# A hybrid decoder block on one core: the residual taken from its normed form, and scatter and weight transposes moved between the gate and the up product

## What is computed

```
def reference(x, ...):
    h = rms_norm(x, g_mix); z = h @ w_in + b_in          # 1024 -> glu a, b | q | k | v | two gates
    y_conv = conformer_conv(glu_a, glu_b, ...)           # 31 causal taps per channel, layer norm, silu, @ w_conv_out
    y_attn = sliding_window_attention(q, k, v, sinks) @ w_attn_out + b_attn_out
    x = x + (gate_conv * y_conv + gate_attn * y_attn) @ w_out
    x = x + moe_ffn(rms_norm(x, g_ffn), ...)
    return rms_norm(x, g_final)

def moe_ffn(h, ...):                                     # 256 tokens, 32 experts, top 4
    logits = hf @ w_router + b_router
    top_v, top_e = lax.top_k(logits, TOP_K); top_w = softmax(top_v)
    ... # tokens sorted by expert; for the rows xblk of expert e:
        g = jnp.minimum(xblk @ w_gate[e] + b_gate[e], 7.0)
        u = jnp.clip(xblk @ w_up[e] + b_up[e], -7.0, 7.0)
        a = (u + 1.0) * (g * jax.nn.sigmoid(1.702 * g))
        yb = a @ w_down[e] + b_down[e]
    y = zeros.at[row_tok].add(yb * row_w)                # scatter, weighted

```

## Time and profile before

| | us |
|---|---|
| median of three runs | 1177.32 |
| the profiled execution, its own time | 1175.85 |
| its span (first to last instruction) | 1174.1 |
| PE busy | 1120.3 (95%) |
| PE weight loads busy | 530.4 (45%) |
| DVE busy | 325.5 (28%) |
| ACT busy | 179.7 (15%) |
| DMA, mean over the span | 376 GB/s, 441.69 MB |

### The profile page before, as it was taken

One profiled execution on the slowest core, in us unless ns is written; L12 is line 12 of the kernel. 1 busy time (PEld: TensorE's weight loads), 2 busy tenths in 40 slices (PEclk: granted clock), 3 DMA queues, 4 the chain that ended last, 5 costly groups with the idle time before them and its releaser, 6 DMA issues.

```text
span 1174.1 us, 13686 instructions
## 1 busy us (share of the span) xinstructions
PE 1120.3 (95%) x5333; PEld 530.4 (45%) x5333; DVE 325.5 (28%) x790; ACT 179.7 (15%) x351; POOL 33.6 (3%) x39
## 2 busy tenths in 40 slices
PE   7999999999999999999999999999999999999997
PEld 6888888854333333333333333333333333333332
DVE  1999973324111111121111111111111111111111
ACT  2111365222011001010011010000000000000011
POOL 2350000000000000000000000000000000000000
PEclk9999999999999999999999999999999999999999
DMA  8966435668999999999999999999999999999996
GB/s 270 349 209 187 143 117 207 251 269 308 408 428 428 433 431 430 429 433 432 433 430 432 430 434 433 431 431 431 430 437 432 431 430 431 434 432 432 431 424 258
DMA packets 54133, 441.69 MB, mean 376 GB/s; under 512 B 4183, under 2 KB 34137, under 8 KB 37336
## 3 DMA queue, kind: packets, MB, share of 16 engines
q1 hardware_dynamic: 53512, 440.20, 90.6%
q0 software_dynamic: 432, 0.95, 0.4%
q10 hardware_dynamic: 160, 0.13, 0.0%
HBM read 440.08 MB, written 1.05 MB: 376 GB/s over the span
## 4 chain that ended last, share of the span: by engine, by line
PE 90%; DMA 5%; another core or an unknown queue 2%; SPq 1%; issue 1%; DVE 0%; ACT 0%; ACTq 0%; DVEq 0%
PE bank L1426 54%; PE bank L1174 17%; PE bank L1394 5%; DMA arena<-in_w_up 4%; PE bank L1379 4%; PE bank L1290 2%; PE bank L1466 2%; PE bank L1436 1%; PE bank L1386 1%; PE bank L1473 1%; DMA arena<-in_g_ffn 1%; PE bank L1197 1%; PE bank L1223 0%; PE bank L1212 0%
## 5 line engine op out<-in xcount | busy, mean ns | idle before, releaser
L1426 PE MATMUL bank<-arena,x_columns 128*64 128x512 f32 x2080 | 468.2, 594 | 26.0 <-DMA arena<-in_w_up 24.5
L1426 PEld LDWEIGHTS bank<-arena,x_columns 128*64 128x64 f32 x2080 | 148.4, 137 | 299.9 <-issue 273.7
L1426 PE MATMUL bank<-arena,act_columns 128*64 128x512 f32 x992 | 219.1, 593 | 11.1 <-DMA arena<-in_w_down 11.1
L1174 PE MATMUL bank<-arena 128*128 128x256 f32 x928 | 205.3, 382 | 1.1 <-DVE arena L779 1.1
L1174 PEld LDWEIGHTS bank<-arena 128*128 128x128 f32 x928 | 176.5, 191 | 27.1 <-issue 1.7
L1426 PEld LDWEIGHTS bank<-arena,act_columns 128*64 128x64 f32 x992 | 76.1, 137 | 150.8 <-issue 150.8
L812 DVE SCALAR_TENSOR_TENSOR arena<-arena x240 | 96.4, 480 | 0.1
L1037 DVE TENSOR_SCALAR bias_selector<-ones_bf,expert_onehot 96x64 bf16<-96x64 bf16 x32 | 7.6, 237 | 270.9 <-PE bank L1386 270.9
L1071 DVE TENSOR_SCALAR gate_clipped<-bank 128x512 f32<-128x512 f32 x32 | 22.1, 692 | 202.8 <-PE bank L1426 202.8
L1075 DVE TENSOR_SCALAR hidden<-bank 128x512 f32<-128x512 f32 x32 | 22.1, 691 | 187.7 <-PE bank L1426 187.7
L1394 PE MATMUL bank<-y_block,scatter 64*128 64x512 f32 x248 | 61.5, 614 | 0.0
(11 more groups left out here) (190 smaller groups left out, 490.0 us busy)
## 6 DMA issues: line engine op xcount, KB each, us to landing
arena<-in_w_up SPq DMA_DIRECT2D x25, 4096.0 KB, 50.7
arena<-in_w_down SPq DMA_DIRECT2D x25, 4096.0 KB, 50.9
arena<-in_w_gate SPq DMA_DIRECT2D x24, 4096.0 KB, 49.9
arena<-in_w_in SPq DMA_DIRECT2D x21, 1024.0 KB, 11.8
arena<-in_w_gate SPq DMA_DIRECT2D x10, 2048.0 KB, 13.0
arena<-in_w_up SPq DMA_DIRECT2D x9, 2048.0 KB, 11.4
arena<-in_w_down SPq DMA_DIRECT2D x8, 2048.0 KB, 15.5
arena<-in_w_down SPq DMA_DIRECT2D x11, 1024.0 KB, 8.7
```

Source lines behind the costliest of these rows:

```text
L1174: last = pe.matmul(bank[n % 3][:, j * T:(j + 1) * T], w[:, c, j * P:(j + 1) * P], src[:, c, :], start=(c == 0), stop=(c == C - 1))
L1426: last = pe.matmul(dst[h * CAP:(h + 1) * CAP, :], lhs(row), cols(rows[:, row, :], h), start=(row == 0), stop=(row == MROWS - 1))
```

## The change

- `add_x` no longer reads x. It multiplies the normed x (`xh`) by a diagonal matrix of its root mean squares (`scales`, two new DVE instructions behind `first_tokensT`). Its four matmuls go to the ends of rounds 3 to 6; `start_y` (round 1) now opens the accumulators.
- So rows 6 and 7 of buffer 5 wait for `xh` alone (`xh_ready`), and their loads stand earlier in SP's queue.
- `first_gather(0)` is cut in two, `ranks(1)` between them. `turn_wts` writes to bank DN in place of B, and the wait for its copy before the first up product is gone.
- In a round, `scatter()` (now of expert b-2) and `turn_weights(b-1)`, into the gather's bank G, stand between gate and up in place of the round's end. ACT's copy of `swT` and DVE's `selw` move with them.
- In the front the vectors' transposes stand in the middle of piece 1, and those of the convolution's weights after piece 2; the DMA of `conv_w` is issued after those of the vectors.
- At the end ACT's squares start per accumulator, and DVE multiplies two accumulators by `g_final` ahead of the scale.
- To make room for `scales`, `before`, `sinks` and the softmax scratch are laid over it.

```diff
...
     for n, col in enumerate(IN_COLS):
         fetch(n, by_cols(n), w_in[:, :, col:col + COLS])
         if n == 1:
-            sp.dma_start(cwrows, t_in["conv_w"]).then_inc(cw_loaded, 16)
             for name, (row, rows) in VEC.items():
                 if name != "g_mix":
                     sp.dma_start(vrows[row:row + rows, :],
                                  t_in[name].rearrange("(c p) -> c p", p=P)).then_inc(vecs_loaded, 16)
+            sp.dma_start(cwrows, t_in["conv_w"]).then_inc(cw_loaded, 16)
             sp.dma_start(wrt, t_in["w_router"].rearrange("(c p) e -> p c e", p=P)).then_inc(wrt_loaded, 16)
...
     first_rows(3, 6, piece_done, WOUT0 + 2)
     first_rows(5, 2, piece_done, WOUT0 + 2)
     first_rows(4, 0, piece_done, WOUT0 + 3)
+    first_rows(5, 6, xh_ready, 1)
     first_rows(4, 2, piece_done, FRONT)
     first_rows(5, 3, piece_done, FRONT)
-    sp.wait_ge(xh_ready, 1)
-    first_rows(5, 6, x_added, 2)
+    first_rows(5, 7, xh_ready, TT)
     for n in range(PAIRS, WHOLES[0]):
-        for k, (lo, hi) in enumerate(parts_of(n)):
-            if n == PAIRS and k == 3:
-                sp.wait_ge(xh_ready, TT)
-                first_rows(5, 7, x_added, 2 * TT)
+        for lo, hi in parts_of(n):
             refill(n, lo, hi)
     with sp.Fori(LOOP0, (WHOLES[-1] + 1) // PAIRS) as cycle:
...
         act.wait_ge(piece_done, done)
         act.activation(dst, src[:], ACT.Copy).then_inc(yb_out, 1)
-    def moe_block(b, then_gather=True, y_before=True, y_after=False, sw=swT, columns=actT):
+    def copy_sw(b, src, sw=swT):
+        act.wait_ge(swT_done, b + 2)
+        act.activation(sw, src[:, 0:T].rearrange("p (t s) -> p t s", t=TT), ACT.Copy).then_inc(swT_out, 1)
+    def moe_block(b, then_gather=True, y_before=True, y_after=False, sw_before=swT, sw_after=False, columns=actT):
         act.wait_ge(gmin_ready, b + 1)
         act.activation(sig, gmin, ACT.Sigmoid, scale=ALPHA).then_inc(sig_ready, 1)
         if not then_gather:
             act.preload_act_table(ACT.Sqrt)
+        if sw_before is not None:
+            copy_sw(b - 1, G, sw_before)
         if then_gather:
             act.wait_ge(act_steps, 2 * b + 1)
...
             copy_y(b * MPE + (FRONT - LEAD + MPE))
         act.wait_ge(actT_done, b + 1)
         act.activation(columns, A[:].rearrange("p (k h s) -> p k h s", k=4, h=2), ACT.Copy).then_inc(actT_out, 1)
-        act.wait_ge(swT_done, b + 2)
-        act.activation(sw, B[:, 0:T].rearrange("p (t s) -> p t s", t=TT), ACT.Copy).then_inc(swT_out, 1)
+        if sw_after:
+            copy_sw(b, B)
         if y_after:
             copy_y(b * MPE + (FRONT + MPE))
-    moe_block(0, y_before=False)
...
         copy_xg(NE)
         with act.Fori(NE, NBLK) as b:
             with act.If(b < n_blocks):
-                moe_block(b, y_before=False, y_after=True)
+                moe_block(b, y_before=False, y_after=True, sw_before=None, sw_after=True)
         act.preload_act_table(ACT.Sqrt)
-    for t in range(TT):
-        act.wait_ge(y_done, t + 1)
-        for h in range(2):
-            if (t, h) == (1, 1):
-                act.wait_ge(gain_on, 1)
-            act.activation((gmin, hidden)[h], Y[t][h][:], ACT.Square, accum_out=ss[:, 2 + h, t:t + 1]).then_inc(squares, 1)
+    def square(t, h):
+        act.wait_ge(y_done, 2 * t + h + 1)
+        if t == 1:
+            act.wait_ge(squares, TT + h + 1)
+        act.activation((gmin, hidden)[h], Y[t][h][:], ACT.Square, accum_out=ss[:, 2 + h, t:t + 1]).then_inc(squares, 1)
+    def y_std(t):
         act.wait_ge(squares_dve, t + 1)
         act.activation(std[:, 0, t:t + 1], ss[:, 1, t:t + 1], ACT.Sqrt, scale=1.0 / D,
                        bias=eps[:, 0:1]).then_inc(stds, 1)
+    square(0, 0)
+    square(0, 1)
+    square(1, 0)
+    y_std(0)
+    act.wait_ge(gain_on, 2)
+    square(1, 1)
+    y_std(1)
     act.wait_ge(rstd_ready, TT)
+    act.wait_ge(gain_on, 2)
     act.activation(ysum[:, 1, 512:], ysum[:, 1, 512:], ACT.Copy, scale=rstd[:, 0, 1:2]).then_inc(last_half, 1)
...
         if then_gather:
             select(b + 1)
+        dv.wait_ge(piece_done, b * MPE + (FRONT - lead + EW))
+        dv.tensor_scalar(gmin, A[:], LIMIT, None, ALU.min).then_inc(gmin_ready, 1)
+        dv.wait_ge(sig_ready, b + 1)
+        dv.tensor_tensor(gmin, gmin, sig, ALU.mult).then_inc(act_steps, 1)
         dv.wait_ge(swT_done, b + 1)
         for t in range(TT):
             last = dv.tensor_scalar(selw[:, t, :], iota[:].rearrange("p a s -> p (a s)"), rank[:, t, bass.ds(b, 1)],
                                     wts[:, t, bass.ds(b, 1)], ALU.is_equal, ALU.mult)
         last.then_inc(selw_ready, 1)
-        dv.wait_ge(piece_done, b * MPE + (FRONT - lead + EW))
-        dv.tensor_scalar(gmin, A[:], LIMIT, None, ALU.min).then_inc(gmin_ready, 1)
-        dv.wait_ge(sig_ready, b + 1)
-        dv.tensor_tensor(gmin, gmin, sig, ALU.mult).then_inc(act_steps, 1)
         dv.wait_ge(piece_done, b * MPE + (FRONT - lead + 2 * EW))
         dv.tensor_scalar(uclip, B[:], LIMIT, -LIMIT, ALU.min, ALU.max).then_inc(act_steps, 1)
...
             tokensT(b + 1)
     first_tokensT()
+    for t in range(TT):
+        dv.tensor_scalar(scales[:, t, :], ident[:], std[:, 1, t:t + 1], None, ALU.mult).then_inc(scales_ready, 1)
     dv.tensor_tensor(le, logits[:, :, 0:NE], m8[:, :, 0:1].to_broadcast([P, TT, NE]), ALU.subtract).then_inc(le_ready, 1)
...
         dv.wait_ge(stds, TT + t + 1)
         dv.reciprocal(rstd[:, 0, t:t + 1], std[:, 0, t:t + 1]).then_inc(rstd_ready, 1)
+    def gained(t, h):
+        cols = slice(h * 512, (h + 1) * 512)
+        dv.tensor_tensor(ysum[:, t, cols], Y[t][h][:], gfin[:, cols], ALU.mult).then_inc(gain_on, 1)
     def half_out(t, h):
         dv.wait_ge(rstd_ready, t + 1)
         cols = slice(h * 512, (h + 1) * 512)
         dv.scalar_tensor_tensor(ysum[:, t, cols], Y[t][h][:], rstd[:, 0, t:t + 1], gfin[:, cols],
                                 ALU.mult, ALU.mult).then_inc(ysum_ready, 1)
-    dv.wait_ge(y_done, 1)
+    dv.wait_ge(gfin_loaded, 16)
+    dv.wait_ge(squares, TT + 1)
+    gained(0, 0)
     sum_of_squares(0)
-    dv.wait_ge(gfin_loaded, 16)
-    dv.wait_ge(y_done, 2)
-    dv.tensor_tensor(ysum[:, 1, 512:], Y[1][1][:], gfin[:, 512:], ALU.mult).then_inc(gain_on, 1)
+    dv.wait_ge(y_done, 2 * TT)
+    gained(1, 1)
     y_rstd(0)
-    half_out(0, 0)
+    dv.wait_ge(rstd_ready, 1)
+    dv.wait_ge(gain_on, 1)
+    dv.tensor_scalar(ysum[:, 0, 0:512], ysum[:, 0, 0:512], rstd[:, 0, 0:1], None, ALU.mult).then_inc(ysum_ready, 1)
+    half_out(0, 1)
     sum_of_squares(1)
-    half_out(0, 1)
     y_rstd(1)
     half_out(1, 0)
...
         pe.matmul(bank[3][:, 0:T], ones[:], ln_sums, start=True, stop=True).then_inc(done, 1)
     project(0, hT, ready=hT_ready, ready_by=1)
+    project(1, hT, (0,))
     pe.wait_ge(vecs_loaded, 16 * (len(VEC) - 1))
     pe.wait_ge(vecs_out, 1)
     pe.transpose(bank[6][:, 0:VROWS], vrows, ident[0:VROWS, 0:VROWS]).then_inc(vecsT, 1)
-    project(1, hT)
+    project(1, hT, (1,))
+    project(2, hT)
     pe.wait_ge(cw_loaded, 16)
     for c in range(C):
         last = pe.transpose(bank[7][:, c * KTAPS:(c + 1) * KTAPS], cwrows[:, c * P:(c + 1) * P],
...
     def add_x(t, h):
-        pe.matmul(Y[t][h][:], ident[:], x[:, t, h * 512:(h + 1) * 512], start=True, stop=False).then_inc(x_added, 1)
+        pe.wait_ge(scales_ready, t + 1)
+        pe.matmul(Y[t][h][:], scales[:, t, :], by_eights(xh[:, t, :])[:, h * CAP:(h + 1) * CAP, :], start=False, stop=False)
...
     router_logits(1, 1)
     router_logits(1, 2)
     sum_of_parts(1)
-    add_x(0, 0)
-    first_gather(0)
+    first_gather(0, range(5))
     ranks(1)
-    add_x(0, 1)
+    first_gather(0, range(5, C))
     first_gather(1)
...
         for t in range(TT):
             for h in range(2):
                 pe.matmul(Y[t][h][:], wT[:, t * P:(t + 1) * P], bdown[:, h * 512:(h + 1) * 512],
-                          start=False, stop=False)
+                          start=True, stop=False)
     def gate_product(b, n, cycle=None):
         if n > 0:
             pe.wait_ge(xT_ready, b + C)
...
                                 ident[:])
         last.then_inc(actT_done, 1)
-    def turn_weights(b):
+    def turn_weights(b, dst):
         pe.wait_ge(selw_ready, b + 1)
         for t in range(TT):
-            last = pe.transpose(B[:, t * P:(t + 1) * P], selw[:, t, :], ident[:])
+            last = pe.transpose(dst[:, t * P:(t + 1) * P], selw[:, t, :], ident[:])
         last.then_inc(swT_done, 1)
-    def round_of(b, n, cycle=None):
+    def round_of(b, n, cycle=None, x_half=None):
         pe.wait_ge(actT_out, b)
         gate_product(b, n, cycle)
+        if n + 2 != 4:
+            pe.wait_ge(yb_out, b - 1)
+            pe.wait_ge(swT_out, b - 1)
+            scatter()
+        turn_weights(b - 1, G)
+        up_product(n + 1, cycle)
         pe.wait_ge(swT_out, b)
-        up_product(n + 1, cycle)
         gather(b + 1)
         if n + 2 == 4:
```

(11 more changed lines are left out.)

69 lines of the change are left out of this document (33 added, 36 removed).

## The result

The changed kernel takes 1179.54 us, the median of 20 runs (1177.94 to 1186.67), the kernel before 1177.19 in 20 runs on the same chip: ratio 1.0031, 95% interval 1.0021 to 1.0041. By the medians it is 2.35 us or 0.2% slower; the ratio takes in all runs, three of which lie at 1186.0 to 1186.7. The interval excludes 1, but the change is at the edge of the 0.3% that the prediction took as no change. The forecast was 1178.4, in a range of 1172 to 1183. The profiled execution takes 1178.93, its span 1177.2 (before 1175.85 and 1174.1), so the two profiles differ by 3.1 us.

The account below looks back on a forecast made before the run. The end was taken as DMA's gapless weight stream plus PE's chain after the last whole matrix. DMA stream -0.3, end +1.0, tail +0.4 gave +1.1 us on 1177.32, so 1178.4 us, range over the cases 1172 to 1183.

Parts of the forecast that it names:

- Lateness of the front: Front: convolution weights' transposes 5.6 us later, DVE 0.96 us in hand, so PE's work from 140.67 on 4.6 us later.
- Head: Start of the experts: saves 1.4 us by gate 0, 3.3 without two add_x, 4.1 by the first up product.
- The DMA stream: Expert weight loads: DMA's delivery changes by -0.3 us, despite refills issued 0.5 us later.
- work in hand: Refills at 299.0: DMA had 2.3 us of work queued, so 0.5 us of lateness only eats into that.
- The prediction's other end: Weight loads if DMA runs dry: stream shifts +0.5 us, and +1.1 where round 2's up product delays its refills.
- Rounds: Expert rounds: PE stands still 1.1 us each, 27.44 us without DMA; PE catches up with 8.7 us to spare.
- End: After the last whole matrix lands: gate 31 starts 1.2 us earlier, scatter and turn follow it; +1.0 us.
- Tail: Last stores: the second sum comes later behind DVE's gains and scale; 0.4 us of this arrives at the last store.
- (a): Front: the taps' lateness doesn't reach PE; 5.9 us less, 1172.5 us; chance 0.13.
- (b): Rounds: PE doesn't catch up and the rounds become PE's; 1184 us at 1.6 us a round; chance 0.13.
- the turning point: Rounds: exposed wait of 1.40 us a round, above which PE would not catch up.
- (c): Weight stream runs thin, DMA dry two or three times for about a microsecond; 1181.5 us; chance 0.12.

Follow-up runs that it names:

- experiment 3: Changed kernel with scatter and weight transposes back at the round's end; new front, x and tail stay: 1177.25 us, ratio 1.0012.
- experiment 9: Changed kernel, old rounds, half of piece 1 before vectors' transpose, convolution weights' transposes right behind piece 1, two idle 128x512 products around first gather: 1171.9 us.
- Experiment 4: Changed kernel with 11 idle products ahead of the layer-norm sum, in PE's wait: 1180.47 us, ratio 1.0029.
- experiment 1: Changed kernel with the front put back as before: 1177.01 us, ratio 0.9989.
- 7: Changed kernel with old rounds, half of piece 1 ahead of the vectors' transpose, convolution weights' transposes right behind piece 1: 1173.75 us, ratio 0.9972.
- 8: Changed kernel with only the convolution weights' transposes moved right behind piece 1: 1176.2 us.
- experiment 11: Changed kernel with x added from adjacent columns of the normed x (wrong order, only times count): 1178.89 us, ratio 1.0033.
- experiment 2: Kernel before with only the new front: 1181.54 us, ratio 1.0039.
- experiment 5: New x, head and tail only, front and rounds as before: 1174.09 us, ratio 0.9973.
- experiment 6: New x, head and tail only, front and rounds as before, plus two idle 128x512 products in the head: 1174.48 us.

## Why the prediction was right, and where its terms were not

The bound was read rightly: the end is the stream's delivery and a fixed chain of PE, and the table above fits that. That time inside the rounds costs nothing while PE has a lead is nearly so: the new rounds moved the mark by 1.1 us (experiment 3). But the total is 1.1 us too low by the medians. Between the profiles the change is 3.1 us where the sum had 1.1: the stream's term is 2.3 too low, the tail's 0.4 too high, the end's right. So the median came nearer to the forecast than the terms behind it did, and one of the steps below was right by luck.

- **Lateness of the front, forecast 4.6.** The weights' transposes came 4.35 us later, not 5.6: the step took piece 0 at the 8.87 us of the profiled run, and a piece can take 7.1 (10.63 for the 48 records of one and a half). In the profiled run of before, products of piece 0 took up to 0.76 us a record where the median is 0.38, beside a granted clock of 1.00; in that of the changed kernel none is over 0.48. It goes with the execution, not the kernel (experiment 9's 12.37), and what it is stays open. The wait, 5.79, was forecast at 5.9, but by luck: the sum came 3.4 late and not 4.6, and PE was 2.4 ahead and not 1.3. What no step held is the clock: 2 us more behind the wait, 5.5 in all. Experiment 4 shows that without the wait the fall is gone.
- **Head, forecast 1.4, 3.3 and 4.1 saved.** 1.2, then 3.9 at up 0. The step was right in kind; with 5.5 us to start from it left 1.6 us at gate 1, not 0.5. What it lacked is that the head without `add_x` can lose the clock (traced in experiments 1, 4, 7 and 8). In the changed kernel's 20 runs such falls seem rare: 17 lie at 1177.9 to 1181.2, three at 1186.0 to 1186.7 with a mean clock of 0.989. That these three fell in the head was not traced.
- **The DMA stream, forecast -0.3.** This is the step that failed: +2.0. It took "work in hand" of DMA as a buffer of 2.3 us against PE's lateness. But between 240 and 440 us the rate was 294, 411 and 428 GB/s where before it was 298, 414 and 431 (50, 50 and 100 us), and about as many bytes again were already missing at 240 us (151 GB/s in place of 166 from 100 to 200 us, where PE stood still), which the step didn't count at all. Nothing makes them good, since DMA is saturated from then on. That the gaps come from PE's later releases is read from the order of work; no single refill was followed. The prediction's other end, +1.1, was nearer.
- **Rounds, forecast 27.44 and 1.1 us of wait.** 27.6 and 1.0 to 1.1. Right. PE catches up before the end, at 1095, with the three weight waits there. `add_x` was to hide in the wait, or cost twice: a product cost twice (1.89, and 1.02 from adjacent columns, experiment 11), and the four rounds with one took 28.2. New rounds cost 2.3 us in all (experiment 3) and 2.5 (8 against 7): 1.0 of it at the end, the rest in the stream.
- **End, forecast +1.0** (its own figures, 1.1 less 0.20, give 0.9). 52.8 against 51.7, and back to 51.7 in experiment 3; gate 31 starts 9.3 us behind the mark (1133.72) for the 9.2 forecast. Right.
- **Tail, forecast +0.4.** Nothing: with old rounds and the new tail the chain is 51.7 as before. The sum of squares stands 4.38 us behind the last scatter's start at 1168.22 where it was 4.1 behind, but the store doesn't come later. The new scale took 0.49 for the 0.5 forecast. The Trainium skill ("VectorE: DVE Perf Modes", The perf-mode tier table) gave an estimate of 0.42; the trace is 0.07 above it and well under the 0.69 of the same operation on a bank, so the doubled rate for float32 within SBUF agrees with this row.

The rivals: (a) was refuted, PE does wait; (b) too, 27.6 is under the 27.74 (26.34 and the turning point of 1.40) from which PE wouldn't catch up; (c) is part of the truth, 411 GB/s and a stream 2 us late, but not the dry stretches it named. Its sign, under 425 GB/s between 300 and 450 us, was no sign: from 300 to 340 us before has 403 and 420, the changed kernel 419 and 399.

By parts, in medians: the new front costs 4.9 us (experiment 2); the new rounds 2.3; the new x, head and tail gain 3.0, and 5.3 between runs with a full clock (1170.7 against 1176.0 for before). Added up that is 4.2 slower, measured is 2.35. The remainder isn't settled; the front's lateness moves the head out of the falls that take experiment 5's gain in half of its runs, which would be of that sign, but why the new head falls seldom when it begins at 275 and nearly always when it begins at 266 is open.

## What to carry to other kernels

Where a saturated stream ends the kernel, count the bytes it has moved when it saturates: a change ahead of that point is worth those bytes, one behind it mostly the chain after the last landing. A step moved later on one engine has to be followed to the next place where another engine takes up its result, however far (here 112 us). And when dense filler work is removed from a stretch of small products with short waits, look at the granted clock of several runs, not of one profile: here the runs of such a kernel split into two groups nearly 6 us apart, half in each (experiment 5).

## What was not expected of the hardware

- A wait of 5.8 us took the granted clock from 1.00 to 0.50; at 144 to 149 us PE worked again and was still at 0.50. It cost about 2 us beyond the wait there (lateness 3.4 to 5.5); that they reach the end isn't shown. With the wait filled down to 0.92 us there was no fall.
- A stretch with waits of only 0.2 to 0.4 us between small products also fell, in the profiles of experiments 1, 4, 7 and 8; in those of the changed kernel and of 3, 5 and 11 the same instructions with the same waits didn't. By the mean clock 6 of 12 runs lay low in experiment 5, 11 of 12 in 7. A fall took 3.3 us at 268 to 276 (22 records 4.22 for 2.79, 16 records 5.50 for 3.65) and in all four profiles was followed by a second one of 1.7 us at the next down product (8.78 for 7.09), 5.0 together; the two groups of experiment 5 are 5.9 us apart (1176.6 against 1170.7). With two idle products two of six runs still lay low.
- The Trainium skill ("TensorE: Matmul & The Clock Gate", A second HAM failure mode: psum-queue depth-cycling) tells of a kernel whose frequent short idles between groups of matmuls make the clock go up and down. The traces agree in part: the falls in the head stand beside waits of 0.2 to 0.4 us only, but the same waits also stand in profiles without a fall. That idle work helps isn't settled: experiment 9 is 1171.9 with it against 1173.75, on another chip; experiment 6 is 1174.48 against 1174.09, where the old front falls too.
- A moving operand read with a stride of eight float32 columns takes nearly twice the time of an adjacent one: 1.03 and 0.59 us for each record of a 128x512 product, 1.89 and 1.02 for the product (its two records). The Trainium skill ("SBUF — State Buffer", Door 1: The DMA port swizzle) has memory lines of 16 bytes, and says that four float32 is how far one can stride for free. The rows agree, with a factor of 1.75 to 1.85.
